# Convolution layers of a six-layer network: gates and values first, z behind them, bias masks moved into these layers

## The chip, the cores and the metric

One core of one Trainium2 chip. The metric is the device time of one launch in microseconds (us), the median of several runs. Engines: PE (TensorE), DVE (VectorE), ACT (ScalarE), POOL (GpSimd), SP (SyncE, which issues all DMAs).

## The reference, cut to what matters

Four mixer layers (convolution a0, forgetting attention b, short convolution c, convolution a1) and then two blocks of sparse and latent attention with a feed-forward part, on 256 tokens, width 1024, inner width 2048, all in float32. The change touches mostly the two convolution layers:

```
def conformer_conv_mixer(h, w_in, conv_w, conv_b, ln_g, ln_b, w_out):
    proj = h @ w_in
    val, glu_gate, z = jnp.split(proj, 3, axis=-1)
    u = val * jax.nn.sigmoid(glu_gate)
    u = causal_depthwise_conv(u, conv_w) + conv_b          # 31 taps
    u = jax.nn.silu(layer_norm(u, ln_g, ln_b))
    return (u * jax.nn.silu(z)) @ w_out
```

The later attention adds a bias looked up by the distance of two positions, `rel_bias[t5_bucket(q_pos - k_pos)]`. It depends on the positions alone, so the kernel builds it early, beside other work.

## The kernel before, in words

**Weights.** All weights stream in one fixed list of pieces of 128x1024 (512 KB) through six raw buffers. A "split" piece is cast by ACT into a high part `wh` (`feed_act`, tile wh), DVE subtracts to get the low part `wl` (`feed_dve`, tile wl), and a unit of PE work is three short-format matmuls of 256 columns for each of 8 row blocks (24 instructions, from XS and wh or wl). A "plain" piece is used by PE as it landed, in full float32: 8 matmuls that the profile shows as 16 instructions (ps<-B,raw). `LOOK = 3`: casts and subtractions run up to three pieces ahead of the unit where they are called for. SP loads piece i once piece i-6 has been used; the queue is in order.

**A convolution layer.** Channels go in eight pairs of 128-channel blocks, p = 0 to 7. For a pair there are two units each of gate (g), value (v) and z. PE makes g and v, ACT takes the sigmoid of g (`gate`), DVE multiplies (`val`, the row B<-ps,tmp), and the 31 taps follow: ACT sets up two of them, 18 are DVE multiply-adds in a PSUM bank (ps<-B,C,ps), and `POOL_TAPS = 11` go by ACT, which scales into one of three buffers (tmp<-B,C), and POOL, which adds (B<-B,tmp). Two instructions for a tap and pair, one for each block. `conv_end` (B<-ps,B) joins both sums. ACT squares the result, PE sums both over the channels (`stats`, the 128x1 matmuls). After pair 7: mean and variance on DVE (`dve_moments`) with one square root on ACT, PE spreads four columns over 128 partitions (`spread`, eight 128x128 instructions), and then DVE normalizes two blocks at a time, ACT applies silu, DVE multiplies with silu(z), ACT and DVE split the result (tile os), and PE multiplies with `w_out` (`pe_out`, 12 matmuls of 512 columns for each of 16 blocks), whose pieces are split in the same loop.

**The order**, written out by hand on each engine: PE does g0 v0, g1 v1, then g_p v_p, the sums of pair p-2 and z_(p-2) for p = 2 to 7, then z6 z7, the last sums, and the spread. g is plain, v plain for even p and split for odd p, z all split: 12 plain and 12 split pairs of units. PE's output goes round four banks, and a unit waits until the bank's last user has been read. ACT and DVE do the taps of pair p-1 in between, in a merged order of 30 items (`items(p, a, b)`; item 0 sets up). ACT loads another function table each time it goes from sigmoid to silu or back.

**The bias.** 96 masks (`masks`, DVE, 128x128), each followed by one small matmul with 32 columns (`pe_bias`, two instructions in the profile); ACT takes out a full bank of 16 (`act_bias`). Masks lie in a ring of six. 32 are made at the very start of the program, before the first layer's norm on DVE and before its transposes on PE; 64 in layer b, four for each pair of key and query units.

Lines: L103 is `matmul`, L106 `transpose`, L109 `activation`, L112 `copy` (the casts), L119 `tt`, L124 `ts`, L129 `stt`, L135 `reciprocal`.

Of the kernel before, what the change touches and what calls it, by code (L numbers as in the profile page):

```python
# [18 lines left out]
E = 2048  # L19
# [8 lines left out]
POOL_TAPS = 11  # L28
# [3 lines left out]
RING = 6  # L32
# [167 lines left out]
def plan_a(j):  # L200
    A, out = f"a{j}", []

    def two(kind, p, base, how):
        for n in range(2):
            out.append((f"{A}.{kind}{p}.{n}", tiles("a_w_in", j, base + p * 256 + 128 * n), how))

    for p in range(9):
        if p < 8:
            two("g", p, E, "plain")
            two("v", p, 0, "plain" if p % 2 == 0 else "split")  # L210
        if p == 8:
            two("z", 6, 2 * E, "split")
            two("z", 7, 2 * E, "split")
        elif p >= 2:
            two("z", p - 2, 2 * E, "split")
# [143 lines left out]
class Net:  # L359
# [85 lines left out]
    def feed_act(self, act, name):  # L445
        s = self.s
        while self.casts <= min(self.at[name] + LOOK, len(self.pieces) - 1):
# [9 lines left out]
    def feed_dve(self, dve, name):  # L457
        s = self.s
        while self.lows <= min(self.at[name] + LOOK, len(self.pieces) - 1):
# [145 lines left out]
    def pe_entry(self, pe, L, normed):  # L605

        s, idn = self.s, self.c("ident", 0, 128)
        self.warm(pe, {"a0": 0, "a1": 14, "b": 14, "c": 14, "m0": 6}.get(L, 20))
# [118 lines left out]
    def a_order(self):  # L727

        seq = []
        for p in range(9):  # L730
            if p < 8:
                seq += [("g", p), ("v", p)]
            seq += [("z", 6), ("z", 7)] if p == 8 else [("z", p - 2)] if p >= 2 else []
        bank = {x: 4 + i % 4 for i, x in enumerate(seq)}
        prior = {x: seq[i - 4] for i, x in enumerate(seq) if i >= 4}
        return bank, prior
# [6 lines left out]
    def pe_a(self, pe, j):  # L743
        s, A = self.s, f"a{j}"
        XN = self.xn()
        if j == 0:
            self.pe_bias(pe, 16, 6)
            self.pe_bias(pe, 16, 7)
# [4 lines left out]
        def pair(kind, p):  # L753
            b = self.ps[bank[kind, p]]
            if j == 0 and p == 1 and kind in "gv":
                pe.wait_ge(*s["evac"]["bias", 0 if kind == "g" else 1])
# [3 lines left out]
            for n in range(2):  # L760
                o = b[:, n * T:n * T + T]
                if kind == "g" or (kind == "v" and p % 2 == 0):
# [11 lines left out]
        for p in range(9):  # L774
            if p < 8:
                pair("g", p)
                pair("v", p)
            else:
                pair("z", 6)
                pair("z", 7)  # L780
            if p >= 2:
                stats(2 * p - 4)
                stats(2 * p - 3)
                if p < 8:
                    pair("z", p - 2)
        stats(14)
        stats(15)
        pe.wait_ge(*s["norm"][(A, "m"), "root"])
        for x in ((k, p) for k, p in bank if bank[k, p] == 7):
            pe.wait_ge(*(s["conv"] if x[0] == "v" else s["evac"])[(A,) + x])  # L790
        self.spread(pe, 7, self.m["sm"][:, 112:116], (A, "m"))
        for k in range(15):
            self.pe_out(pe, A, k, 16)
        self.pe_out_last(pe, A, [15])

    def act_a(self, act, j):
# [4 lines left out]
        if j == 0:  # L801
            self.act_rms(act, A, lambda tb, h: s[f"x{tb}"][0], "a_norm0", True)
            self.act_bias(act, 0, 6)
            self.act_bias(act, 1, 7)
# [58 lines left out]
        for p in range(9):  # L863
            at = 12 if p - 1 >= 2 else 0
            if p < 8:
                for n, (kind, m) in enumerate((("g", 0), ("g", 1), ("v", 0), ("v", 1))):
                    self.feed_act(act, f"{A}.{kind}{p}.{m}")
                    if p >= 1:
                        items(p - 1, min(30, at + 6 * n), min(30, at + 6 * n + 6))
                    if n == 1:  # L870
                        gate(p)
                if p >= 1:
                    items(p - 1, min(30, at + 24), 30)
            else:
                for n, (q, m) in enumerate(((6, 0), (6, 1), (7, 0), (7, 1))):
                    self.feed_act(act, f"{A}.z{q}.{m}")
                    items(7, min(30, at + 6 * n), min(30, at + 6 * n + 6))
                    if m:
                        silu_z(q)
                items(7, min(30, at + 24), 30)  # L880
            if p >= 2:
                stats(2 * p - 4)
                stats(2 * p - 3)
                if p < 8:
                    for m in range(2):
                        self.feed_act(act, f"{A}.z{p - 2}.{m}")
                        items(p, 6 * m, 6 * m + 6)
                    silu_z(p - 2)
# [4 lines left out]
        act.table(ACT.Silu)  # L893
        for i in range(0, 22, 2):
# [5 lines left out]
            if 2 <= i < 18:  # L900
                for k in (i - 2, i - 1):
# [3 lines left out]
                    self.act_high(act, A, k, V[:, k, :])  # L905
            for k in (i - 4, i - 3):
                if 0 <= k < 16:
                    self.feed_act(act, f"{A}.o{k}")

    def dve_a(self, dve, j):  # L910
# [4 lines left out]
        if j == 0:  # L915
            self.dve_bias_begin(dve)
            self.masks(dve, 32)
# [46 lines left out]
        for p in range(9):  # L964
            at = 12 if p - 1 >= 2 else 0
            if p < 8:
                for n, (kind, m) in enumerate((("g", 0), ("g", 1), ("v", 0), ("v", 1))):
                    self.feed_dve(dve, f"{A}.{kind}{p}.{m}")
                    if p >= 1:
                        items(p - 1, min(30, at + 6 * n), min(30, at + 6 * n + 6))  # L970
                if p >= 1:
                    items(p - 1, min(30, at + 24), 30)
                val(p)
            else:
                for n, (q, m) in enumerate(((6, 0), (6, 1), (7, 0), (7, 1))):
                    self.feed_dve(dve, f"{A}.z{q}.{m}")
                    items(7, min(30, at + 6 * n), min(30, at + 6 * n + 6))
                items(7, min(30, at + 24), 30)
            if p >= 1:
                conv_end(p - 1)  # L980
            if 2 <= p < 8:
                for m in range(2):
                    self.feed_dve(dve, f"{A}.z{p - 2}.{m}")
                    items(p, 6 * m, 6 * m + 6)
        self.dve_moments(dve, 2, E, 1e-6, s["sums"][A, 15], (A, "m"))
        dve.wait_ge(*s["spread"][A, "m"])
        mu = self.ps[7][:, 0:T].unsqueeze(1).to_broadcast([128, 2, T])
        R = self.ps[7][:, T:2 * T].unsqueeze(1).to_broadcast([128, 2, T])
        for i in range(0, 22, 2):
            if i < 16:  # L990
# [3 lines left out]
                dve.tt(a, a, R, ALU.mult).then_inc(s["norm"].up((A, "ln", i // 2)), 1)  # L994
            if 2 <= i < 18:
# [99 lines left out]
    def mask(self, n):  # L1095
        i = n % RING
        b = self.m["B"][2][:, 3392:3776] if i < 3 else self.m["sc"]
        return b[:, (i % 3) * 128:(i % 3) * 128 + 128]
# [11 lines left out]
    def masks(self, dve, n):  # L1110
# [3 lines left out]
        for _ in range(n):  # L1114
# [3 lines left out]
            if x >= RING:  # L1118
                dve.wait_ge(*s["table"][x - RING])
# [3 lines left out]
    def pe_bias(self, pe, n, bank):  # L1123
# [3 lines left out]
        for _ in range(n):  # L1127
# [3 lines left out]
            if x > 32 and x % 16 == 0:  # L1131
# [65 lines left out]
    def pe_b(self, pe):  # L1197
# [27 lines left out]
        for which in ("k", "q"):  # L1225
            for n, i in enumerate(range(0, 16, 2)):
# [11 lines left out]
                self.pe_bias(pe, 4, 3)  # L1238
# [56 lines left out]
    def act_b(self, act):  # L1295
# [23 lines left out]
        for which, dst in (("k", K), ("q", Q)):  # L1319
            for n, i in enumerate(range(0, 16, 2)):  # L1320
                if n and n % 4 == 0 or (which == "q" and n == 0):
                    self.act_bias(act, (3 if which == "q" else 2) + (1 if n and which == "q" else 0), 3)
# [12 lines left out]
        self.act_bias(act, 5, 3)  # L1335
# [32 lines left out]
    def dve_b(self, dve):  # L1368
# [72 lines left out]
        for st in range(19):  # L1441
# [1072 lines left out]
```

## Time and profile before

| | |
|---|---|
| median of 3 runs | 1984.69 us (1981.28 to 1985.75) |
| the profiled execution's own time | 1980.45 us |
| its span | 1978.7 us |
| PE busy | 1893.4 us, 96% |
| DVE busy | 1471.1 us, 74% |
| ACT busy | 1081.7 us, 55% |
| POOL busy | 308.3 us, 16% |
| mean granted clock of PE | 0.974 |

Times in rows are us from the span's start. A timeline row gives start, length, engine, line, operation, tiles out<-in, shape, count, and in brackets the idle time before it and what ended that. Matmuls overlap, so the time that one group costs PE is read from its start to the next group's start. The layers lie at: a0 from 0 to 260, b to 627, c to 862, a1 to 1108.

### The profile page before, as it was taken

How to read it: one execution, taken by the hardware profiler on the slowest of the kernel's cores; microseconds unless marked ns; L12 is line 12 of the kernel's file. 1: busy time of each engine (PE TensorE's matmuls, PEld its weight loads, DVE VectorE, ACT ScalarE, POOL GpSimd, SP SyncE). 2: the span in 40 equal slices, each digit the busy share in tenths (PEclk: the TensorE clock that was granted, in tenths of full speed). 3: DMA queues.
4: the chain of work that ended last, by engine and by line, in shares of the span. 5: the costliest groups of instructions: out<-in, count | busy, mean ns of one | idle time of the engine just before them, and what ended most of it. 6: DMA issues, size and time to landing. Idle time of an engine off the chain costs nothing.

```text
span 1978.7 us, 32775 instructions
## 1 busy us (share of the span) xinstructions
PE 1893.4 (96%) x12594; PEld 1718.5 (87%) x12594; DVE 1471.1 (74%) x2798; ACT 1081.7 (55%) x1936; POOL 308.3 (16%) x380
## 2 busy tenths in 40 slices
PE   9899899999999999998997999999999999999997
PEld 8898678887888999988996888889999898889996
DVE  7999766565676888769997677677777676677667
ACT  5788464333435444457885544546455545555554
POOL 2888000000000000008781000002000200002000
PEclk9899799998999999998997999999999999999999
DMA  5335356553444788854343454354665343445552
GB/s 210 128 139 172 115 182 224 189 166 135 148 144 165 272 300 293 302 167 153 134 171 110 162 199 147 118 186 133 220 229 176 138 144 118 137 141 175 208 190 76
DMA packets 93899, 342.23 MB, mean 173 GB/s; under 512 B 10416, under 2 KB 10672, under 8 KB 93104
## 3 DMA queue, kind: packets, MB, share of 16 engines
q1 hardware_dynamic: 93744, 340.14, 50.6%
q8 instruction: 100, 1.64, 0.3%
q14 instruction: 55, 0.45, 0.1%
HBM read 339.05 MB, written 1.05 MB: 172 GB/s over the span
## 4 chain that ended last, share of the span: by engine, by line
PE 74%; DVE 15%; ACT 9%; issue 2%; POOL 0%; DMA 0%; SPq 0%; DVEq 0%; ACTq 0%
PE ps L103 72%; DVE ps L129 5%; DVE wl L119 5%; ACT tmp L109 4%; ACT wh L112 2%; PE ps L106 1%; DVE B L119 1%; ACT B L109 1%; DVE tmp L119 1%; ACT ps L109 1%; ACT XS L112 0%; DVE X L129 0%; DVE tmp L129 0%; DVE X L119 0%; ACT os L112 0%
## 5 line engine op out<-in xcount | busy, mean ns | idle before, releaser
L103 PE MATMUL ps<-XS,wh 128*128 128x256 f32 (+1 forms) x5072 | 940.4, 287 | 4.4 <-DVE wl L119 3.2
L103 PEld LDWEIGHTS ps<-XS,wh 128*128 128x128 f32 (+1 forms) x5072 | 802.1, 193 | 12.0 <-ACT wh L112 3.5
L119 DVE TENSOR_TENSOR wl<-raw,wh 128x1024 fp32r<-128x1024 f32 (+1 forms) x493 | 601.1, 1246 | 198.6 <-ACT wh L112 198.1
L103 PE MATMUL ps<-XS,wl 128*128 128x256 f32 (+1 forms) x2536 | 722.2, 285 | 0.0
L112 ACT CAST wh<-raw 128x1024 fp32r<-128x1024 f32 (+1 forms) x493 | 494.6, 1038 | 89.1 <-PE ps L103 87.0
L103 PEld LDWEIGHTS ps<-XS,wl 128*128 128x128 f32 (+1 forms) x2536 | 490.1, 193 | 0.0
L119 POOL TENSOR_TENSOR B<-B,tmp 128x236 f32<-128x236 f32 (+10 forms) x352 | 268.3, 802 | 777.7 <-ACT tmp L109 777.7
L103 PE MATMUL ps<-wh,os 128*128 128x512 f32 x864 | 286.4, 400 | 14.3 <-DVE os L119 11.7
L129 DVE SCALAR_TENSOR_TENSOR ps<-B,C,ps 128x254 f32<-128x254 f32 (+17 forms) x576 | 224.4, 466 | 8.4 <-ACT ps L109 8.3
L103 PEld LDWEIGHTS ps<-wh,os 128*128 128x128 f32 x864 | 165.8, 192 | 50.6 <-DVE os L119 12.9
L103 PE MATMUL ps<-wl,os 128*128 128x512 f32 x432 | 171.5, 397 | 0.0
L103 PE MATMUL ps<-B,raw 128*128 128x256 f32 x768 | 168.2, 379 | 0.0
L103 PEld LDWEIGHTS ps<-B,raw 128*128 128x128 f32 x768 | 145.1, 190 | 19.2
L119 POOL TENSOR_TENSOR X<-X,B 128x512 f32<-128x512 f32 x24 | 39.8, 1675 | 706.7 <-DVE XS L119 705.8
L109 ACT ACTIVATE tmp<-B,C 128x236 f32<-128x236 f32 (+10 forms) x352 | 142.7, 477 | 8.7 <-POOL B L119 8.2
L109 ACT ACTIVATE B<-ps 128x512 f32<-128x512 f32 (+2 forms) x92 | 53.4, 586 | 164.4 <-PE ps L103 163.8
L129 DVE SCALAR_TENSOR_TENSOR tmp<-ps,C,tmp 128x254 f32<-128x254 f32 (+1 forms) x176 | 72.7, 475 | 77.4 <-ACT tmp L109 77.2
L109 ACT ACTIVATE tmp<-ps 128x384 f32<-128x384 f32 (+2 forms) x129 | 65.7, 516 | 117.1 <-PE ps L103 83.3
L129 DVE SCALAR_TENSOR_TENSOR raw<-raw,cb 128x1024 f32<-128x1024 f32 x96 | 116.3, 1216 | 0.0
L109 ACT ACTIVATE tmp<-ps,C 128x256 f32<-128x256 f32 x88 | 44.9, 561 | 120.3 <-PE ps L103 120.3
L103 PE MATMUL ps<-wh,XS 128*128 128x512 f32 x320 | 100.1, 391 | 0.0
L103 PEld LDWEIGHTS ps<-wl,os 128*128 128x128 f32 x432 | 83.2, 193 | 14.9
(157 smaller groups left out, 1855.4 us busy)
## 6 DMA issues: line engine op xcount, KB each, us to landing
raw<-in_w SPq DMA_DIRECT2D x623, 512.0 KB, 4.3
raw<-in_w SPq DMA_DIRECT2D x12, 384.0 KB, 3.7
B<-in_ln SPq DMA_DIRECT2D x4, 1024.0 KB, 6.8
C<-in_cst SPq DMA_DIRECT2D x1, 1109.5 KB, 10.3
X<-in_x SPq DMA_DIRECT2D x2, 512.0 KB, 6.1
out_x<-X SPq DMA_DIRECT2D x4, 256.0 KB, 2.5
cb<-in_cb SPq DMA_DIRECT2D x1, 512.0 KB, 12.7
raw<-in_w SPq DMA_DIRECT2D x2, 256.0 KB, 3.2
```

The costliest lines, as they stand in the source:

```text
L103: return NOTHING if self.e is None else self.e.matmul(*a, **k)
L106: return NOTHING if self.e is None else self.e.transpose(*a)
L109: return NOTHING if self.e is None else self.e.activation(*a, **k)
L112: return NOTHING if self.e is None else self.e.copy(*a)
L119: return NOTHING if self.e is None else self.e.tensor_tensor(o, a, b, op)
L129: return self.e.scalar_tensor_tensor(out=o, in0=a, scalar=s, in1=b, op0=op0, op1=op1, **k)
```

## The change

Order of the pieces and of PE in the convolution layers: g_p v_p for p = 0 to 7 and then z0 to z7. Only v0 is a plain value now, and z0 to z3 are plain. `POOL_TAPS` is 12. The sums of pair q come after v_(q+3) (one pair later than before), z6 runs between the last sums and the spread, and z7 behind the spread. The value of pair p+1 and the taps' setup no longer wait for the end of pair p's taps. 16 masks are made at the start instead of 32, 32 in a0 after the norm, 16 in layer b's attention, 32 in a1 after the norm; PE multiplies 16 of them at the start, eight after each of v1 to v4 in both convolution layers, and 16 at the start of c in place of 14 warming matmuls. Masks lie in the buffer that z will use.

```
-POOL_TAPS = 11
+POOL_TAPS = 12
+PLAIN_Z = 4
...
+    for p in range(8):
+        two("g", p, E, "plain")
+        two("v", p, 0, "split" if p else "plain")
+    for p in range(8):
+        two("z", p, 2 * E, "plain" if p < PLAIN_Z else "split")
...
+        if L == "c":
+            self.pe_bias(pe, 16, 7)
+        self.warm(pe, {"a0": 0, "a1": 14, "b": 14, "c": 0, "m0": 6}.get(L, 20))
...
         if j == 0:
             self.pe_bias(pe, 16, 6)
-            self.pe_bias(pe, 16, 7)
...
+        for p in range(8):
+            pair("g", p)
+            pair("v", p)
+            if 1 <= p < 5:
+                self.pe_bias(pe, 8, 3)
+            if p >= 3:
+                stats(2 * p - 6)
+                stats(2 * p - 5)
+        for p in range(6):
+            pair("z", p)
+            if p in (1, 4, 5):
+                q = {1: 5, 4: 6, 5: 7}[p]
+                stats(2 * q)
+                stats(2 * q + 1)
+        pair("z", 6)
         pe.wait_ge(*s["norm"][(A, "m"), "root"])
...
+        pe.wait_ge(*s["evac"][A, "z", 3])
         self.spread(pe, 7, self.m["sm"][:, 112:116], (A, "m"))
+        pair("z", 7)
```

On ACT (DVE has the same pattern, with `val(p + 1)` after item 20, `conv_end(p - 1)` after item 8, and `masks(32)` ahead of the first value):

```
+        gate(0)
+        self.feed_act(act, f"{A}.v1.0", 1)
+        for p in range(8):
+            items(p, 0, 4)
+            if p < 6:
+                self.feed_act(act, f"{A}.v{p + 2}.0", 0)
+            if p in (2, 4):
+                self.act_bias(act, (4 if j else 1) + (p == 4), 3)
+            if p == 7:
+                silu_z(2)
+                self.feed_act(act, f"{A}.z4.0", 1)
+            items(p, 4, 10)
+            if p < 7:
+                gate(p + 1)
+            else:
+                silu_z(3)
+                self.feed_act(act, f"{A}.z5.0", 1)
+            items(p, 10, 14)
...
+            if p == 6:
+                silu_z(0)
+            items(p, 14, 18)
+            if p:
+                stats(2 * p - 2)
+                stats(2 * p - 1)
+            items(p, 18, 22)
+            if p == 6:
+                silu_z(1)
...
+        silu_z(4)
+        self.feed_act(act, f"{A}.z7.0", 0)
         stats(14)
         stats(15)
...
+        self.feed_act(act, f"{A}.z7.1", 0)
+        silu_z(5)
+        self.feed_act(act, f"{A}.o0", 1)
+        silu_z(6)
...
+            if i == 4:
+                silu_z(7)
```

In the output loop of DVE `feed_dve(o0, i // 2)` is added for i = 0 and 2: the first pieces of `w_out` used to be split before the loop. Layer b loses `pe_bias(4, 3)`, `masks(4)` and four `act_bias`, and gets `masks(4)` for the heads 9 to 12 between `maxima` and `dve_quotients`.

## Rows read from the trace of the kernel before

**Rows 1.** The page, part 4: the chain that ended last, by engine.

```profile
PE 74%; DVE 15%; ACT 9%; issue 2%; POOL 0%; DMA 0%; SPq 0%; DVEq 0%; ACTq 0%
```

**Rows 2.** Windows: stretch, busy PE, PEld, DVE, ACT, POOL, granted clock, DMA share, GB/s.

```profile
882.30:1048.10 165.80, 154.40 (x1008) 145.88 (x1006) 154.49 (x330) 135.30 (x289) 134.12 (x176) 0.96 0.43 150
66.10:76.30 10.20, 8.19 (x38) 8.19 (x39) 8.62 (x22) 6.69 (x18) 6.79 (x12) 0.50 0.13 50
376.70:383.50 6.80, 6.80 (x33) 6.80 (x33) 5.99 (x12) 0.89 (x1) 0.00 (x0) 0.50 0.91 317
```

**Rows 3.** Timeline of PE in a0: sums, a split pair, two plain pairs.

```profile
91.67 0.50 PE L103 MATMUL ps<-C,B 128*128 128x1 f32 x4
...
93.37 0.48 PE L103 MATMUL ps<-XS,wh 128*128 128x256 f32 x2
...
99.21 13.98 PE L103 MATMUL ps<-B,raw 128*128 128x256 f32 x64
```

**Rows 4.** Timeline of PE in a1: first units; spread; output.

```profile
868.25 20.88 PE L103 MATMUL ps<-B,raw 128*128 128x256 f32 x96
...
1053.45 2.07 PE L103 MATMUL ps<-C,sm 128*128 128x128 f32 x8 [1.73 <-DVE sm L129]
1060.22 0.80 PE L103 MATMUL ps<-wh,os 128*128 128x512 f32 x1 [4.70 <-DVE os L119]
```

**Rows 5.** Timeline of the program's start on PE, DVE and ACT.

```profile
4.12 1.46 PE L103 MATMUL ps<-C,B 128*128 128x32 f32 x6 [4.12 <-DVE B L124]
...
17.98 3.65 PE L106 MATMUL ps<-C,tmp 128*128 128x128 f32 x16
...
3.63 0.85 DVE L124 TENSOR_SCALAR B<-B,C 128x128 f32<-128x128 f32 x3
...
15.70 0.16 DVE L124 TENSOR_SCALAR sm<-sm 128x2 f32<-128x2 f32 x1
...
29.36 0.34 DVE L124 TENSOR_SCALAR rope<-rope,C 32x256 f32<-32x256 f32 x1
...
9.75 0.19 ACT L109 ACTIVATION_READ_ACCUMULATOR tmp<-X 128x1 f32 x1
```

**Rows 6.** Timeline of DVE in a1: first pair's taps, then a low part.

```profile
884.35 13.80 DVE L129 SCALAR_TENSOR_TENSOR ps<-B,C,ps 128x254 f32<-128x254 f32 x36 [0.26 <-ACT ps L109]
...
903.34 1.67 DVE L119 TENSOR_TENSOR wl<-raw,wh 128x1024 fp32r<-128x1024 f32 x1 [0.45 <-ACT wh L112]
```

**Rows 7.** Timeline of POOL in a1: the adds of pairs 0 and 1.

```profile
885.52 14.07 POOL L119 TENSOR_TENSOR B<-B,tmp 128x236 f32<-128x236 f32 x22 [685.72 <-ACT tmp L109]
901.30 15.97 POOL L119 TENSOR_TENSOR B<-B,tmp 128x236 f32<-128x236 f32 x22 [1.71 <-ACT tmp L109]
```

**Rows 8.** Timeline of ACT in a1: table for silu, (silu left out), cast, scaled taps.

```profile
1008.27 1.28 ACT L109 ACT_TABLE_LOAD   x1
...
1010.06 1.04 ACT L112 CAST wh<-raw 128x1024 fp32r<-128x1024 f32 x1
1010.99 1.62 ACT L109 ACTIVATE tmp<-B,C 128x232 f32<-128x232 f32 x4
```

**Rows 9.** Timeline of DVE in the output loop of a0.

```profile
208.99 2.73 DVE L119 TENSOR_TENSOR B<-B,ps 128x512 f32<-128x512 f32 x4 [2.17 <-PE ps L103]
...
223.09 0.76 DVE L119 TENSOR_TENSOR os<-B,os 128x256 fp32r<-128x256 f32 x2 [0.86 <-ACT os L112]
...
253.38 0.76 DVE L119 TENSOR_TENSOR os<-B,os 128x256 fp32r<-128x256 f32 x2 [0.47 <-ACT os L112]
```

**Rows 10.** Timeline of PE in layer b: sums, next sums; then the mask wait.

```profile
342.22 1.04 PE L103 MATMUL ps<-tmp,C 128*16 128x256 f32 x4
...
350.03 1.04 PE L103 MATMUL ps<-tmp,C 128*16 128x256 f32 x4
...
376.38 0.86 PE L103 MATMUL ps<-C,sc 128*128 128x32 f32 x4 [1.80 <-DVE sc L124]
```

**Rows 11.** Timeline of DVE in layer b's attention: the wait where masks go.

```profile
547.96 0.17 DVE L135 RECIPROCAL sm<-sm 128x2 f32<-128x2 f32 x1 [0.98 <-ACT tmp L109]
```

More of the change, by code:

```diff
@@ L443, in sp_program, with feed_act @@
         sp.wait_ge(s["out"].sem, 64)
-    def feed_act(self, act, name):
+    def feed_act(self, act, name, look=LOOK):
         s = self.s
-        while self.casts <= min(self.at[name] + LOOK, len(self.pieces) - 1):
+        while self.casts <= min(self.at[name] + look, len(self.pieces) - 1):
             i = self.casts
@@ L727, in a_order @@
     def a_order(self):
[L729 to L733, printed above, removed]
+        seq = [(kind, p) for p in range(8) for kind in "gv"] + [("z", p) for p in range(8)]
         bank = {x: 4 + i % 4 for i, x in enumerate(seq)}
         prior = {x: seq[i - 4] for i, x in enumerate(seq) if i >= 4}
+        bank["z", 7], prior["z", 7] = 4, ("z", 4)
         return bank, prior
@@ L754, in pair @@
             b = self.ps[bank[kind, p]]
-            if j == 0 and p == 1 and kind in "gv":
-                pe.wait_ge(*s["evac"]["bias", 0 if kind == "g" else 1])
+            if j == 0 and p == 1 and kind == "g":
+                pe.wait_ge(*s["evac"]["bias", 0])
             if (kind, p) in prior:
@@ L761, in pair @@
                 o = b[:, n * T:n * T + T]
-                if kind == "g" or (kind == "v" and p % 2 == 0):
+                if kind == "g" or (kind, p) == ("v", 0) or (kind == "z" and p < PLAIN_Z):
                     self.plain_unit(pe, o, f"{A}.{kind}{p}.{n}", XN, A)
@@ L861, in stats @@
                 s["square"].up((A, i)), 1)
[L863 to L873, printed above, removed]
-            else:
[L875 to L888, printed above, removed]
+        gate(0)
[12 more added lines that the diff above has]
+                gate(p + 1)
+            else:
+                silu_z(3)
+                self.feed_act(act, f"{A}.z5.0", 1)
+            items(p, 10, 14)
+            if p < 6:
+                self.feed_act(act, f"{A}.v{p + 2}.1", 0)
+            if p == 6:
[7 more added lines that the diff above has]
+                silu_z(1)
+            if p == 7:
+                self.feed_act(act, f"{A}.z6.0", 0)
+            items(p, 22, 30)
+        silu_z(4)
+        self.feed_act(act, f"{A}.z7.0", 0)
         stats(14)
@@ L962, in val @@
                    ALU.mult).then_inc(s["conv"].up((A, "v", p)), 1)
[L964 to L979, printed above, removed]
-                conv_end(p - 1)
[L981 to L984, printed above, removed]
+        self.masks(dve, 32)
+        self.feed_dve(dve, f"{A}.v1.0", 1)
+        val(0)
+        for p in range(8):
+            items(p, 0, 8)
+            if p:
+                conv_end(p - 1)
+            if p < 6:
+                self.feed_dve(dve, f"{A}.v{p + 2}.0", 0)
+            if p == 7:
+                self.feed_dve(dve, f"{A}.z4.0", 1)
+            items(p, 8, 14)
+            if p == 7:
+                self.feed_dve(dve, f"{A}.z5.0", 1)
+            items(p, 14, 20)
+            if p < 7:
+                val(p + 1)
+            if p < 6:
+                self.feed_dve(dve, f"{A}.v{p + 2}.1", 0)
+            items(p, 20, 28)
+            if p == 7:
+                self.feed_dve(dve, f"{A}.z6.0", 0)
+            items(p, 28, 30)
+        conv_end(7)
+        self.feed_dve(dve, f"{A}.z7.0", 0)
         self.dve_moments(dve, 2, E, 1e-6, s["sums"][A, 15], (A, "m"))
+        self.feed_dve(dve, f"{A}.z7.1", 0)
         dve.wait_ge(*s["spread"][A, "m"])
```

59 lines of the change are left out of this document (17 added, 42 removed).

## The prediction

> **What bounds the kernel now.** I read the chain of waits by engine first: PE holds three quarters of the chain, DVE a seventh [rows 1]. The windows by stage then show where PE isn't the bound: in the taps' stretch of a convolution layer PE and DVE are both busy 154 of 165.8 us and POOL 134 [rows 2]. The timeline of PE shows what DVE and ACT cost it at the end of the layer, 1.73 us before the spread and 4.70 before the output [rows 4]; a window of a0 with 2.0 of 10.2 us idle is wholly at half clock [rows 2], as are others behind pauses. So a gain comes from filling these pauses with z, as long as the taps on DVE, ACT and POOL end in time, and from work that PE no longer does. I work with the profiled execution, 1980.45 us; it lies 4.2 under the median of the runs, so gains are taken off the median at the end.
>
> **Prices on PE.** A split pair of units costs 5.84 us, start to start, after a plain one about 5.9; a plain pair 6.90 (two take 13.98, overlap of 0.17 left out); the sums of a pair 1.70 [rows 3]. In layer b the period is 7.81 [rows 10], of which 5.9 are units and 1.0 are the norm's sums; the four masks' matmuls have the rest, 0.9.
>
> **Layer b.** 16 groups of four masks' matmuls go. 15 of them give 0.9 each, 13.5. The sixteenth stands behind the 1.80 us wait for a mask, and after it PE runs at half clock for 6.8 us [rows 2, 10], which costs 3.4: with the matmuls themselves (about 1.0 at that clock) 6.2, less 0.3 that PE will then wait for the low part of the next units. Sum 19.4. ACT loses four evacuations and DVE 64 masks there; both have slack. The 16 masks that come back in the attention stand where DVE now waits 0.98 us for ACT [rows 11]; four masks take 4 x 0.26 = 1.04 (0.85 for three that overlap [rows 5]). Hidden but for 0.1 a head if DVE has no other slack; all of it, 4.2, if it has none; I take 0.4. Layer b: 19.0 less time; bounds 14 and 20. In c, 16 masks' matmuls (3.6 us at 0.9 for four) replace 14 warming ones of about the same length: 0, between -1 and +1; ACT's one more evacuation hides behind PE's split units.
>
> **The start of a0.** 32 masks' matmuls hold PE from 4.12 to 17.98, 0.43 each [rows 5]. 16 end at 11.1. The norm could start when ACT has its squares, 9.75 + 0.19, but DVE makes masks until 15.70 [rows 5]; with 16 masks it is ready at 3.6 + 16 x 0.26 = 7.8. The norm comes 5.8 us earlier, and so PE's first unit, now at the end of the transposes, 21.4: 15.6. If the full clock comes no earlier than now, PE runs its first units at half speed until about 21.7 and loses 3.0; if it comes as long after the transposes as now, nothing. I take 1.5. But DVE now makes 32 masks (8.2) and two low parts (2.4) before it multiplies the first value: norm and rope are done at 29.7 - 5.8 = 23.9 [rows 5], so the first value is ready at 35.2, against 36.3 now. Of the 5.8 us PE keeps all, the taps 1.1. In a1 the masks fit where DVE idles while PE makes g0 and v0, but for about 0.5.
>
> **PE's ledger of a convolution layer.** Now 12 plain and 12 split pairs, then 13 and 11: +1.0. The masks' matmuls add eight groups of four at 0.85: +6.8. From the first unit to the end of z3: 13 plain pairs 89.7, seven split 41.3, six sums 10.2, masks 6.8: 148.0. From there z4 5.9, sums 1.7, z5 5.9, sums 1.7, z6 5.9, spread 1.0.
>
> **The taps.** DVE: 36 multiply-adds take 13.80 [rows 6], 34 take 13.0; value and join 1.2; two low parts of 1.2 to 1.67 [rows 6]: about 17 a pair against 20.7 now (165.8 / 8 [rows 2]). POOL: 22 adds take 14.07 with no low part in between, 0.64 each, and 15.97 with two, so a low part on DVE costs POOL 0.95 [rows 7]. 24 adds and two low parts: 15.4 + 1.9 = 17.3. The Trainium skill, SBUF — State Buffer, section "SBUF: two separate sides", says that DVE operations with two SBUF inputs and POOL operations shut each other out for a whole instruction. By that rule a low part would cost POOL all its 1.22 or so, and a layer's 17 low parts 4.6 us more than by the rows; I keep the rows.
> ACT: 24 scaled taps at 0.39 [rows 8], 9.3, setup 2.1, gate 0.6, two casts 1.9, squares 0.7: 14.6. It loses about 11 table loads of 1.28 [rows 8] a layer, since the gates are together. So POOL and DVE set 17.3 a pair, and POOL is ready for pair 7 at: a1, first add 0.5 later than 885.52 [rows 7], + 6 x 17.3 + 15.4 (pair 6 has no low part) = 1005.
>
> **What is late next.** In pair 7 ACT waits for silu of z2 after item 4 and of z3 after item 10, in order, ahead of the taps that POOL needs. In a1 PE starts at 868.3 [rows 4], so z3 ends at 868.3 + 148.0 = 1016.3, 11 us after POOL could start pair 7. Then ACT: silu 0.5, two casts 1.9, the next scaled taps 0.8 [rows 8]: 1019.5. POOL has 16 adds and three low parts left: 10.2 + 2.9 = 13.1, so 1032.6. Join 0.7, the rest of the squares and PE's sums 2.0: 1035.3; z6 5.9, spread 1.0: the layer norm starts at 1042.2. Now it starts at 1053.45 + 2.07 = 1055.5 [rows 4]. Gain 13.3. In a0 the same chain from 15.6 + 1.5 + 148.0 = 165.1 gives 191.0 against 208.99 [rows 9]: 18.0.
>
> **The output loop.** PE has z7 for the 4.70 us pause, and the half clock behind it goes. But the first splits of w_out moved into DVE's loop: one at i = 0, one at i = 2, three instead of two at i = 4, 1.2 each, and ACT has silu of z7 and one more cast at i = 4. Followed through, the third pair of os comes 4.1 later than 223.09 - 208.99 = 14.1 behind the norm's start, and the period after it stays 6.4, as now. The last pair starts 44.4 + 4.1 = 48.5 behind it [rows 9]; with its first half's 0.4 and two blocks on PE (2 x 2.72 at full clock) the output ends at 54.3. Now it ends at 51.4 (PE's 16 blocks from 4.7 on, 3.2 of it lost to half clock). Cost 2.9 a layer; between 0, if PE sets the end, and 4.4.
>
> **Sum.** Layer b 19.0, a0 18.0 - 2.9, a1 13.3 - 2.9: 44.5. 1980.45 - 44.5 = 1936.0, and 1984.69 - 44.5 = 1940.2 for the median. Its own range, from the bounds above: 1930 to 1951.
>
> **Rivals.** (A) PE alone sets the pace: ACT's stall in pair 7 is covered by what POOL still has buffered. Then the norm starts at PE's ledger, 148.0 + 22.1 after the first unit: 1038.4 and 187.2, 3.8 less each: 1932.6. For it: three buffers between ACT and POOL. Against: they hold 3 x 1.3 us of adds, the stall is 11.
> (B) Half clock at the tail. PE pauses about 4 us before the last sums of a1 (ready at 1031, taps done at 1033.5) and 1 to 3 in the output loop. The pause of 1.80 was followed by 6.8 us at half clock, and 10.2 is the longer kind [rows 2, 10]. Two such stretches a layer, 4 us each at the end: +8 to +16, 1952. The Trainium skill, TensorE: Matmul & The Clock Gate, section "What's actually happening", has it that the engine is throttled by default and activity releases it; by this rule the pauses count, the trace agrees.
> (C) Slower than before: the half clock comes with every pair. PE's 14.6 to 15.5 us of work a pair lie inside a tap period of 17.3, and if the slack is taken as one pause of 2 us before each pair's sums, and each brings 10.2 us at half clock (5.1 lost), 12 of them cost 61: 2002. It decides from nine such pauses on (44.5 / 5.1). Against: in a1 PE starts behind the taps and reaches each sum later than they do.
> (D) Layer b gives less: with the masks gone PE waits at the same place for low parts or weights (three pieces of 512 KB in 7 us are 225 GB/s, under the 317 of a busy stretch [rows 2]). Then only 8 of its 19 us come: 1951.
> (E) The start gives nothing, since PE waits for the taps anyway: +4; within the range.
>
> **How the numbers follow.** The forecast 0.5, A 0.2, B 0.18, C 0.03, D 0.07, others above 1960 0.02. The range takes in A with the lower bounds of the output loop and of layer b (1932.6 - 2 x 2.9 - 1 = 1926, and 2 for the start's clock: 1924) and B with its 16 us and the upper bound of the attention's masks (1956 + 4): 1924 to 1960. About 0.2% (4 us) is what a measurement of this kernel can tell from no change. Faster 0.95, same 0.02, slower 0.03.
>
> **What would show it.** Right: layer b's key and query period on PE 6.9 instead of 7.81 and no 1.80 wait; first unit on PE near 15.6; the start of the layer norm near 191 in a0 and near 1042.2 - 34 = 1008 in a1 (a0 and b come first); on ACT an idle stretch before the silu of z2 and z3 in pair 7, and on POOL idle time there in place of the idle time at each pair's start; the output loop's end 54 behind the norm's start. Wrong: half clock inside the taps' stretch (C), POOL's adds above 0.75 each throughout, or PE waits on low parts in layer b (D).

## The result and the profile after the change

| | before | after |
|---|---|---|
| median | 1984.39 us (4 runs, 1981.28 to 1985.75) | 1957.32 us (4 runs, 1951.40 to 1963.19) |
| the profiled execution | 1980.45 us | 1957.44 us |

The ratio is 0.9866, 95% interval 0.9834 to 0.9898: 27 us faster by the medians, 23 by the two profiled executions. The forecast was 44.5, to 1940.2. By stages of the two profiled executions, each from the last stage's end to its own:

| stage | forecast | measured | short of the forecast |
|---|---|---|---|
| a0, to the end of its output (260.34, now 254.33) | -15.1 | -6.0 | 9.1 |
| b (to 627.16, now 602.75) | -19.0 | -18.4 | 0.6 |
| c | 0 | 0.0 | 0 |
| a1 (862.14 to 1106.94, now 837.73 to 1081.09) | -10.4 | -1.4 | 9.0 |
| the two blocks behind | 0 | +2.7 | 2.7 |

So both convolution layers lack 9 us. The windows of the kernel after show where: first the two stretches from the first unit to the end of z3 (where z4 starts), then those at half clock inside them and the one before a0's spread. Columns as in [rows 2].

```profile
15.30:172.98 157.68, 155.85 (x914) 143.33 (x913) 144.38 (x340) 119.70 (x275) 124.23 (x175) 0.96 0.43 139
843.84:999.72 155.88, 154.62 (x915) 142.37 (x913) 140.07 (x328) 116.24 (x272) 123.77 (x175) 0.96 0.41 132
...
75.80:82.60 6.80, 6.80 (x26) 6.08 (x26) 6.80 (x17) 6.37 (x15) 6.80 (x11) 0.50 0.00 0
96.30:103.10 6.80, 6.80 (x21) 5.72 (x21) 6.80 (x16) 4.69 (x12) 6.80 (x11) 0.50 0.00 0
901.90:912.10 10.20, 10.20 (x36) 9.03 (x36) 10.20 (x23) 8.06 (x20) 10.20 (x14) 0.50 0.01 2
925.80:929.20 3.40, 3.40 (x10) 2.65 (x9) 3.40 (x7) 2.46 (x8) 3.40 (x5) 0.51 0.00 0
191.90:195.30 3.40, 3.40 (x18) 3.40 (x18) 1.42 (x6) 3.26 (x5) 0.00 (x0) 0.50 0.77 245
```

From first unit to z4 PE takes 157.7 and 155.9 where the prediction had 149.5 and 148.0. 13.6 us at half clock in each cost half of that, 6.8. The timeline of PE in the kernel after shows the rest: the start; the masks' matmuls behind v3, where the bank of 16 is full until ACT takes it out; those behind v4; the last sums; and the spread and the output.

```profile
3.90 7.01 PE L103 MATMUL ps<-C,B 128*128 128x32 f32 x32 [3.90 <-DVE B L124]
...
15.30 7.02 PE L103 MATMUL ps<-B,raw 128*128 128x256 f32 x26
...
73.89 2.63 PE L103 MATMUL ps<-C,B 128*128 128x32 f32 x20 [1.83 <-ACT B L109]
...
93.51 2.29 PE L103 MATMUL ps<-C,B 128*128 128x32 f32 x20
95.66 0.58 PE L103 MATMUL ps<-C,tmp 128*128 128x1 f32 x4
96.11 0.81 PE L103 MATMUL ps<-C,B 128*128 128x1 f32 x4
...
189.24 0.61 PE L103 MATMUL ps<-C,B 128*128 128x1 f32 x4 [2.63 <-DVE B L119]
...
198.37 1.05 PE L103 MATMUL ps<-C,sm 128*128 128x128 f32 x8
206.01 0.50 PE L103 MATMUL ps<-wh,os 128*128 128x512 f32 x1 [0.84 <-DVE os L119]
```

To be seen: the first unit stands at 15.30 against 21.4 [rows 5]. The half clock from 75.8 on stands just behind the pause that ends at 73.89; the stretch from 96.3 on has no pause ahead of it, only eight masks' matmuls and the sums (93.51 to 97.6). a1 has the same pair: 1.25 us of waiting for ACT at 900.62, half clock from 901.9 and again from 925.8. The 1.73 and 4.70 of [rows 4] are gone; in their place PE waits 2.63 for the last join of the taps, at 189.24 and at 1015.98, and 0.84 before the output.

POOL in pairs 6 and 7 of a0, kernel after:

```profile
151.91 5.10 POOL L119 TENSOR_TENSOR B<-B,tmp 128x232 f32<-128x232 f32 x8 [2.53 <-ACT tmp L109]
158.81 3.79 POOL L119 TENSOR_TENSOR B<-B,tmp 128x228 f32<-128x228 f32 x6 [1.81 <-ACT tmp L109]
...
169.40 4.73 POOL L119 TENSOR_TENSOR B<-B,tmp 128x236 f32<-128x236 f32 x6 [5.05 <-ACT tmp L109]
176.31 12.05 POOL L119 TENSOR_TENSOR B<-B,tmp 128x233 f32<-128x233 f32 x16 [2.18 <-ACT tmp L109]
```

and ACT, the silu of z2 and of z3, which stand ahead of the scaled taps that POOL lacks:

```profile
166.46 0.60 ACT L109 ACTIVATE B<-ps 128x512 f32<-128x512 f32 x1 [3.13 <-PE ps L103]
...
173.36 0.60 ACT L109 ACTIVATE B<-ps 128x512 f32<-128x512 f32 x1 [2.13 <-PE ps L103]
```

In layer b the 1.80 us wait of [rows 10] is gone; one of 0.50 for a low part is left. The sums of two key and query units stand at 346.42 and 353.33, 6.9 apart against 7.81:

```profile
346.42 1.04 PE L103 MATMUL ps<-tmp,C 128*16 128x256 f32 x4
353.33 1.04 PE L103 MATMUL ps<-tmp,C 128*16 128x256 f32 x4
...
362.06 0.47 PE L103 MATMUL ps<-XS,wh 128*128 128x256 f32 x2 [0.50 <-DVE wl L119]
```

### The profile page after: what moved, and what is told of

The parts are those of the page before. It is cut to its first block, busy times and chain, and to the rows that moved or that the text cites. A ratio compares the mean times of both kernels' runs of the same rounds, so it can differ in the third digit from the quotient of the medians.

```text
span 1955.6 us, 32679 instructions
## 1 busy us (share of the span) xinstructions
PE 1889.9 (97%) x12534; PEld 1707.9 (87%) x12534; DVE 1451.4 (74%) x2762; ACT 1067.0 (55%) x1944; POOL 314.4 (16%) x412
## 4 chain that ended last, share of the span: by engine, by line
PE 74%; DVE 11%; ACT 8%; issue 5%; POOL 1%; DMA 0%; SPq 0%; DVEq 0%; ACTq 0%; POOLq 0%
PE ps L103 73%; DVE wl L119 4%; ACT tmp L109 3%; ACT wh L112 2%; POOL B L119 1%; DVE B L119 1%; PE ps L106 1%; ACT B L109 1%; DVE tmp L119 1%; DVE B L124 1%; ACT os L112 1%; DVE tmp L129 0%; DVE X L129 0%; ACT XS L112 0%; ACT ps L109 0%
## 5 line engine op out<-in xcount | busy, mean ns | idle before, releaser
L103 PE MATMUL ps<-XS,wh 128*128 128x256 f32 (+1 forms) x5008 | 927.1, 287 | 4.9 <-DVE wl L119 3.7
L103 PEld LDWEIGHTS ps<-XS,wh 128*128 128x128 f32 (+1 forms) x5008 | 790.4, 193 | 18.2 <-issue 7.5
L103 PE MATMUL ps<-XS,wl 128*128 128x256 f32 (+1 forms) x2504 | 711.9, 284 | 0.0
L103 PEld LDWEIGHTS ps<-XS,wl 128*128 128x128 f32 (+1 forms) x2504 | 482.8, 193 | 0.0
L119 POOL TENSOR_TENSOR B<-B,tmp 128x237 f32<-128x237 f32 (+11 forms) x384 | 274.4, 755 | 740.2 <-ACT tmp L109 740.2
L129 DVE SCALAR_TENSOR_TENSOR ps<-B,C,ps 128x254 f32<-128x254 f32 (+16 forms) x544 | 211.9, 471 | 21.6 <-ACT ps L109 21.2
L103 PE MATMUL ps<-B,raw 128*128 128x256 f32 x832 | 194.2, 395 | 0.0
L103 PEld LDWEIGHTS ps<-B,raw 128*128 128x128 f32 x832 | 164.2, 199 | 23.6
L109 ACT ACTIVATE tmp<-B,C 128x237 f32<-128x237 f32 (+11 forms) x384 | 160.6, 478 | 32.6 <-POOL B L119 32.2
```

Of the source, the lines that this page charges most:

```text
L103: return NOTHING if self.e is None else self.e.matmul(*a, **k)
L109: return NOTHING if self.e is None else self.e.activation(*a, **k)
L119: return NOTHING if self.e is None else self.e.tensor_tensor(o, a, b, op)
L129: return self.e.scalar_tensor_tensor(out=o, in0=a, scalar=s, in1=b, op0=op0, op1=op1, **k)
```

## The experiments

The medians below were taken in groups, each beside the kernel before on the same chip (medians 1982.5, 1984.7 and 1983.5; the last repeat with 11 taps stands alone, one execution beside one of 1984.3); ratios are to that. Each trace is of one execution.

**The base.** No edit.

> The changed kernel once more, unchanged, as the base for the runs beside it. Expected 1957 (1951 to 1963), by every theory. In the profile: two stretches at half clock between the first value and the end of z3 in each convolution layer, and one pause of 1 to 2 us of PE for ACT before the third group of masks' matmuls.

Median 1956.2 (1953.7 to 1964.9), ratio 0.9856 (0.9836 to 0.9876). Pauses for ACT of 2.54 and 1.37, half clock at 74.5 and 98.4, 910.8 and 931.2: the pattern repeats, but not the lengths. Half clock takes 10.2 and 6.8 us in a0 here and 6.8 and 6.8 in a1, where the first trace had 6.8 and 6.8, and 10.2 and 3.4.

**The masks' matmuls elsewhere.** On PE they move from behind v_p to between g_p and v_p, one pair later. Theories 1 to 3 are told in the expectation.

```
+            if 2 <= p < 6:
+                self.pe_bias(pe, 8, 3)
             pair("v", p)
-            if 1 <= p < 5:
-                self.pe_bias(pe, 8, 3)
```

> The masks' matmuls of the convolution layers move from behind v1 to v4 to between g and v of the pairs 2 to 5. ACT has then taken out the first bank long before PE wants it, and the masks' matmuls no longer stand directly ahead of the channel sums. Theory 1 (the missing time is what the masks' matmuls bring with them: a pause for ACT of 1.83 and 1.25 us and stretches at half clock, 13.6 us of them in each layer, behind the pause and behind masks and sums in one run): the stretches between first value and z3 go, z3 ends at 164.3 in a0 instead of 172.98, and the kernel gains 1.83 + 6.8 + 1.25 + 6.8 = 16.7, less 0 to 4 if the taps then set the end: 1941 to 1945. Theory 2 (only the pause brings half clock, and the second stretch comes from the taps' work or the time since the start): the second stretch stays, 3.4 and 1.7 us, gain about 11: 1946. Theory 3 (the placing of the masks' matmuls does nothing; PE is slower there for the weights' stream or the taps): the stretches stay, gain 0 to 3: 1954 to 1957.

Median 1963.2 (1956.0 to 1976.7), ratio 0.9899 (0.9871 to 0.9928): no gain, rather a loss, which none of the three theories had. The pauses for ACT went, but PE now waits for low parts: 5.67 at 74.05, 2.19 at 124.87, 0.51 at 141.55, and 2.18 and 3.28 in a1. The wait of 5.67 stands behind one low part that took 9.08 us on DVE (last section), so a0 of this execution says little; a1 has none such. From the first unit to z4 a0 took 160.1 and a1 156.0, where the kernel after had 157.7 and 155.9. So in a1 something else than the pause holds PE in this stretch.

**The bank taken out sooner.**

```
+            if p in (2, 4):
+                self.act_bias(act, (4 if j else 1) + (p == 4), 3)
             items(p, 0, 4)
             if p < 6:
                 self.feed_act(act, f"{A}.v{p + 2}.0", 0)
-            if p in (2, 4):
-                self.act_bias(act, (4 if j else 1) + (p == 4), 3)
```

> Only ACT's taking out of the bias bank moves: at the start of pairs 2 and 4 ahead of the first four tap items and the casts instead of behind them. The pause of PE before the third group of masks' matmuls (1.83 in a0, 1.25 in a1) goes or is halved; the run of thin matmuls (eight masks, then the sums of a pair) stays. Theory 1 (such a run alone is followed by half clock): the stretches stay, perhaps shorter by 3.4 us each, gain 2 to 6: 1951 to 1955. Theory 2 (the pause brings the half clock): the stretch behind the pause goes in both layers, gain 1.8 + 1.3 + 3.4 + 5.1 = 11.6: 1946.

Median 1956.1 (1953.8 to 1958.9), ratio 0.9859 (0.9838 to 0.9880): nothing gained, which neither theory had. Both pauses for ACT are gone, and at their places half clock still comes, 3.4 us in a0 and 6.8 in a1. The kernel after had 6.8 and 10.2 there, its repeat 10.2 and 6.8; so half clock comes without the pause, and what the pause adds is not shown by one trace each. The second stretch of a0 now begins at 136.0, inside a wait of PE. In v6 and v7 of a0 new waits stand, PE's timeline:

```profile
119.12 0.47 PE L103 MATMUL ps<-XS,wh 128*128 128x256 f32 x2 [2.02 <-DVE wl L119]
136.44 0.76 PE L103 MATMUL ps<-XS,wh 128*128 128x256 f32 x2 [2.65 <-DVE wl L119]
```

This gave **theory L**: up to v7 PE is tied to DVE. The second low part of v(p+2) is made behind the value of pair p+1, at item 20 of pair p, so it keeps the taps' pace. What PE saves is spent waiting there, as soon as PE is ahead of it.

**The order alone, masks as before.** Ring of six, 32 at the start, `pe_bias(4, 3)` back in layer b, none in a0's and a1's loops. This undoes one half of the change.

> Only the new order of the convolution layers and the 12 taps; bias masks, their matmuls and their evacuations where they were before (32 at the start, 64 in layer b, ring of six). Layer b is as before (+18.4), PE's first unit at 21.4 instead of 15.3 and the first value near 36.3 instead of 34.1. Theory L (until z3 PE is held by the second low parts of v6 and v7, which stand in DVE's queue behind the value of the next pair; the masks' matmuls, their pause and their half clock only fill time in which PE would have waited): the convolution layers hardly gain from losing the masks, z3 ends at 173 to 175 in a0 and 155 after the first unit in a1, PE waits 2 to 8 us for low parts in v5 to v7; 1957 + 18.4 + 2 - 3 = 1974 (1970 to 1978). The prediction's ledger (PE's own work alone): masks' matmuls 6.8, pause and half clock about 8 less in each layer, 14 to 15 gained in a1 and 9 in a0: 1957 + 18.4 - 24 = 1951.

Median 1975.2 (1972.1 to 1977.0), ratio 0.9948 (0.9928 to 0.9968): theory L had 1974, the ledger alone 1951. So the new order and the twelfth tap alone gain 9.5 beside their own kernel before, and some 17 to 18 of the 27 come from the moved masks. PE's timeline in a0, every row with a wait between 86 and 142 us:

```profile
88.69 0.47 PE L104 MATMUL ps<-XS,wh 128*128 128x256 f32 x2 [2.65 <-DVE wl L120]
106.00 0.47 PE L104 MATMUL ps<-XS,wh 128*128 128x256 f32 x2 [2.65 <-DVE wl L120]
123.31 0.47 PE L104 MATMUL ps<-XS,wh 128*128 128x256 f32 x2 [2.64 <-DVE wl L120]
140.62 0.47 PE L104 MATMUL ps<-XS,wh 128*128 128x256 f32 x2 [2.64 <-DVE wl L120]
```

and DVE beside it, without an idle row:

```profile
103.72 0.68 DVE L120 TENSOR_TENSOR B<-ps,tmp 128x512 f32<-128x512 f32 x1
104.32 1.54 DVE L120 TENSOR_TENSOR wl<-raw,wh 128x1024 fp32r<-128x1024 f32 x1
105.78 7.86 DVE L130 SCALAR_TENSOR_TENSOR ps<-B,C,ps 128x243 f32<-128x243 f32 x20
113.55 0.68 DVE L120 TENSOR_TENSOR B<-ps,B 128x512 f32<-128x512 f32 x1
114.15 1.60 DVE L120 TENSOR_TENSOR wl<-raw,wh 128x1024 fp32r<-128x1024 f32 x1
115.67 5.43 DVE L130 SCALAR_TENSOR_TENSOR ps<-B,C,ps 128x250 f32<-128x250 f32 x14
121.03 0.67 DVE L120 TENSOR_TENSOR B<-ps,tmp 128x512 f32<-128x512 f32 x1
```

The waits are 17.31 apart, as the values on DVE are: PE's slack is taken once in each pair, in front of one low part. The masks' matmuls in the changed kernel mostly fill this time.

**The second low part sooner**, on top of the early evacuation; on DVE:

```
             if p == 7:
                 self.feed_dve(dve, f"{A}.z5.0", 1)
+            if p < 6:
+                self.feed_dve(dve, f"{A}.v{p + 2}.1", 0)
             items(p, 14, 20)
             if p < 7:
                 val(p + 1)
-            if p < 6:
-                self.feed_dve(dve, f"{A}.v{p + 2}.1", 0)
```

> The kernel with ACT's early evacuation of the bias bank (the pause of PE for ACT is gone in it, and PE waits 2.0 and 2.65 us for low parts in v6 and v7 of a0 instead), and on DVE the second low part of v(p+2) at item 14 of pair p instead of behind the value at item 20, about 3 us sooner. Theory L (low parts hold PE until z3): these waits go, z3 ends 2.5 to 3 us sooner in a0 and 0.4 to 1.5 in a1, and with it silu of z3, the taps' end and the norm: 1956 - 3 to 5 = 1951 to 1953. If the clock or the taps' own pace held PE there: the waits turn into others, 1955 to 1957.

Median 1948.7 (1946.4 to 1955.7), ratio 0.9824 (0.9802 to 0.9846): 7 us less than without the moved low part, more than the 3 to 5 expected. By the traces the stretch to z4 is 3.7 shorter in a0 (156.5 to 152.8) and 2.9 in a1 (153.4 to 150.45). a0 has no wait for a low part any more, a1 two of 1.13. In a1 the last unit of v7 follows its low part at once in both kernels, at 962.01 and now at 959.08 with the same first unit, so the half clock of 10.2 that a1 had without the moved low part had only filled time of waiting. Its windows from first unit to z4, and the two stretches at half clock in a0:

```profile
15.33:168.17 152.84, 152.84 (x913) 140.81 (x913) 143.07 (x340) 119.69 (x275) 124.27 (x175) 0.97 0.44 144
842.59:993.04 150.45, 148.19 (x915) 136.98 (x913) 139.18 (x328) 116.50 (x272) 123.85 (x175) 1.00 0.43 137
...
73.50:80.30 6.80, 6.80 (x22) 5.72 (x22) 6.80 (x14) 6.67 (x17) 6.43 (x9) 0.50 0.00 0
94.00:97.40 3.40, 3.40 (x9) 2.65 (x10) 3.40 (x9) 3.24 (x8) 3.40 (x6) 0.50 0.00 0
```

**Silu later on ACT.** z0 moves to item 22 of pair 6, z1 to item 10 of pair 7, z2 behind the taps, z3 and z4 behind the root:

```
-                silu_z(2)
                 self.feed_act(act, f"{A}.z4.0", 1)
...
-                silu_z(3)
+                silu_z(1)
                 self.feed_act(act, f"{A}.z5.0", 1)
...
             if p == 6:
-                silu_z(1)
+                silu_z(0)
...
-        silu_z(4)
+        silu_z(2)
         self.feed_act(act, f"{A}.z7.0", 0)
...
+        silu_z(3)
         self.feed_act(act, f"{A}.z7.1", 0)
+        silu_z(4)
```

> ACT takes silu of z0 to z4 later (z0 at item 22 of pair 6, z1 at item 10 of pair 7, z2 behind pair 7's taps, z3 and z4 behind the norm's root), so that no scaled tap is queued behind a z unit of PE. By the prediction's step (ACT's stall in pair 7 sets the end of the taps): the waits of ACT of 2 to 3 us go, POOL's idle time of 11.6 us in pairs 6 and 7 of a0 goes, the last sums no longer wait for DVE (2.63 in each layer) and the half clock behind that pause (3.4 us, 1.7 lost) goes too: 4.3 a layer, 1957 - 8.6 = 1948 to 1949. By the rival (the taps themselves are too slow, POOL's and DVE's own 17.3 us a pair): the join of pair 7 stays where it is, the pause of 2.6 us too, gain 0 to 2: 1955 to 1957.

Median 1948.9 (1946.0 to 1949.8), ratio 0.9820 (0.9799 to 0.9840): 7.3 less than the base, as the prediction's step had it. The last sums start without a wait in both layers, and the half clock before the spread is gone. POOL's idle time in pairs 6 and 7 of a0, which was to go, only fell from 12.0 to 7.4. But this execution has one low part of 9.10 us on DVE (last section), behind which PE waited 4.66 at 73.63; z3 ended late because of it and the norm still began 1 us sooner than in the kernel after.

**All of it**, and the two first low parts of `w_out` ahead of the norm's loop:

```
+        self.feed_dve(dve, f"{A}.o0", 1)
         dve.wait_ge(*s["spread"][A, "m"])
...
-            if i < 4:
-                self.feed_dve(dve, f"{A}.o0", i // 2)
```

> All of it: silu of z later (alone 1949), early evacuation of the bias bank, second low parts at item 14, and the two first low parts of w_out ahead of the layer norm's loop instead of inside it. Theory L: z3 3 us sooner in a0 and 1 in a1, but the taps' own pace then sets the end (17.3 a pair, seven pairs and 13 us from the first add), so 0 to 3 a layer of it show; the output loop 2.4 to 3.5 shorter in each layer, 54.9 to 52. Sum 1949 - 6 - 2 = 1941 (1937 to 1945). If a low part on DVE is again held up for 5 to 9 us by POOL's adds: up to 5 more, 1946.

Median 1937.5 (1936.6 to 1942.4), ratio 0.9767 (0.9745 to 0.9790): 18 us under the changed kernel by the two ratios, 47 under the one before. The moved low parts of `w_out` had little part in it, 0.7 a layer where 2.4 to 3.5 was expected. From the spread to the output's end it is, in a0, 189.94 to 245.22, 55.3, against 56.0. DVE's timeline in a0 says why:

```profile
188.02 1.23 DVE L119 TENSOR_TENSOR wl<-raw,wh 128x1024 fp32r<-128x1024 f32 x1 [2.09 <-ACT wh L112]
189.94 2.36 DVE L119 TENSOR_TENSOR wl<-raw,wh 128x1024 fp32r<-128x1024 f32 x2 [0.70 <-ACT wh L112]
192.22 2.72 DVE L119 TENSOR_TENSOR B<-B,ps 128x512 f32<-128x512 f32 x4
```

ACT's first cast for them is done only at 189.9, when PE's spread is already starting; the two low parts no longer stand inside the loop but directly ahead of it.

**A gap for DVE on POOL**, on top of all of it:

```
+                if p < 6 and k in (8, 5):
+                    pool.wait_ge(*s["low"][self.at[f"{A}.v{p + 2}.{int(k == 5)}"]])
```

> As the one with all of it, and POOL waits before its fourth and seventh tap of the pairs 0 to 5 until DVE has made the low part that stands there. Theory S (a low part on DVE gets no turn while POOL's adds follow each other without a gap: one took 9.10 us in one run, in which POOL did 12 adds on end): with the wait every low part of these pairs takes 1.2 to 1.7 us, none over 2. POOL idles about 1.2 for each, little more than the 0.95 it loses now: 0 to 4 us slower or faster than without, 1938 to 1945. Rival (the long low part came from the weights' stream or a late cast): long ones can appear here too.

Median 1937.5 (1936.4 to 1941.9), ratio 0.9767 (0.9745 to 0.9788). The same time, and no long low part in the convolution layers, but the kernel without the wait had none either: it costs nothing and shows nothing.

**11 taps.** `POOL_TAPS = 11` in the changed kernel.

> The changed kernel with 11 taps on ACT and POOL, as before the change, so that DVE makes 18 multiply-adds for each block instead of 17. Theory L (DVE's time for a pair is the pace, 17.3, and PE follows it through the low parts): a pair takes 2 x 0.38 more, 18.1; PE gets waits for low parts and the norm starts 5 to 6 later in each layer: 1957 + 10 to 12 = 1967 to 1969. If POOL set the pace, a pair gets shorter (two adds of 0.64 less) and the kernel 0 to 8 faster: 1950 to 1957. If PE's own work set it: 1957, no change.

Median 1961.6 (1952.2 to 1967.2), ratio 0.9899 (0.9878 to 0.9919); the profiled execution is the one of 1952.2. In it a pair of taps takes 17.3 from value to value, as with 12. My 18.1 was wrong: with 11 taps POOL has some slack (it waits 1.21 for ACT at 104.94), and DVE's low parts mostly take 1.2 to 1.35 instead of 1.45 to 1.65:

```profile
99.44 1.21 DVE L119 TENSOR_TENSOR wl<-raw,wh 128x1024 fp32r<-128x1024 f32 x1
...
108.78 1.20 DVE L119 TENSOR_TENSOR wl<-raw,wh 128x1024 fp32r<-128x1024 f32 x1
```

Of what the two added multiply-adds cost, 0.8, the shorter low parts give back 0.4 to 0.6; DVE's idle time for ACT in three of the pairs of the kernel after (0.67 to 1.30) is gone too. So the twelfth tap did not change the pace in this execution. The median is another matter: it lies between what the three theories had, 5 us over the base's 1956.2 and 8.5 by the ratios, and the pace doesn't explain that.

**Repeats for the long low part.** The kernel with silu later unchanged, the same with POOL waiting (as above, before taps 8 and 3), and the one with 11 taps again.

> The kernel with silu of z later, once more, unchanged, to see whether its one low part of 9.10 us on DVE (pair 1 of a0, DVE in line behind 12 of POOL's adds) comes again. Time as before, 1949 (1946 to 1952). If the place decides, a low part of over 5 us stands at the same place in this profile; if it hangs on the moment in which DVE and POOL meet, it may be gone or elsewhere.

> The same, and POOL waits for the low part in the pairs 0 to 5 before the tap that stands beside it, which gives DVE a gap between two adds. If POOL's row of adds is what holds the low part up: none of over 2 us in the pairs 0 to 5, 1945 to 1950. If something else holds it up (a late piece of weights, a late cast), a long one can appear all the same.

> The kernel with 11 taps once more. Its profiled execution took 1952.2, the four others 1961 to 1967. If the difference comes from low parts on DVE that get no turn beside POOL's adds, an execution near 1961 shows one or more of over 5 us in the convolution layers, which the one at 1952 did not (longest 1.7); if it comes from half clock or from the weights' stream, the low parts are all short and the clock's list or the stretches of other layers are longer.

Silu later again: 1946.0 (2 runs), no low part over 1.8 in the convolution layers: the place alone does not decide. With the gap: 1945.1 (2 runs), none either, which shows nothing of the gap. 11 taps again: 1954.75, longest 3.10 at 91.59. None caught an execution near 1961, so the 9 to 15 us by which four of the executions with 11 taps were longer stay unexplained.

## Why the prediction was right in direction and too large

The measured 1957.3 lies in the range, 1924 to 1960, at its upper end, 17 over the forecast of 1940.2. That it lies inside is in part luck: the width on that side was kept for half clock at the tail, and two other things used it.

**The sum of PE's work was right; what held PE was not only its work.** The ledger had 148.0 from first unit to z4. Time less waits and less half of what ran at half clock (with the low part sooner the full clock came at 15.5, so a0's start lost nothing):

| kernel, layer | taken | waits | clock | left |
|---|---|---|---|---|
| after, a0 | 157.7 | 1.8 | 6.8 + 1.2 at the start | 147.9 |
| after, a1 | 155.9 | 1.25 | 6.8 | 147.8 |
| low part sooner, a0 | 152.8 | 0 | 5.1 | 147.7 |
| low part sooner, a1 | 150.45 | 2.3 | 0 | 148.2 |
| order only, a1 (no masks: 148.0 - 6.8 = 141.2) | 152.6 | 10.9 | 0 | 141.7 |

The step that failed is "From the first unit to the end of z3 ... 148.0" as the time at which z3 ends; it took 157.7 and 155.9. It left out two things. First, v6's and v7's low parts, which stand in DVE's queue behind five pairs of taps at 17.3: with the bank taken out sooner PE waited for them in a0 (2.65 at 136.44), and z4 could not come before about 136.4 + 2.9 + 1.7 + 14.0 + 1.7 + 14.0 = 170.7, where I had 165.1. Of a0's 7.9 us at z4, 5.6 would thus have been lost without any pause or half clock. In a1 the same sum from 962.01 gives 996.3, 5.7 later than 148.0 behind the first unit at 842.6. The text named low parts as a risk for layer b only, in (D). Second, the masks' matmuls at 0.85 for four, with nothing around them: they brought pauses of 1.83 and 1.25 for ACT, and behind them 6.8 us were lost at half clock in each layer. Without these matmuls (order only) a1 had no half clock in this stretch and a0 3.4 us. These two aren't added: each fills time that the other would take, which is why removing the pauses alone gave nothing (1956.1), and only together with the low part 7 us. Why the clock falls at the masks' matmuls stays open.

**Layer b, right.** 18.4 for 19.0; period 6.9, no 1.80, and one wait of 0.50 for a low part where I had 0.3. **c, right**, 0.0. **The start of a0, right**: first unit 15.30 for 15.6, first value 34.09 for 35.2, clock lost 1.2 for 1.5.

**The taps' pace, right in size, wrong in its reason.** 17.3 on POOL and DVE alike; with 11 taps it is 17.3 too. The rows of DVE in the order-only kernel show it without an idle row at 12 taps, so a low part's extra 0.3 to 0.4 beside POOL counts on DVE, where I had it on POOL only.

**ACT's stall in pair 7, right.** From z4 to the norm's start a1 took 26.4 for the predicted 25.9. With silu later it took 22.1 in both layers (a0: 176.4 to 198.47), exactly rival A's chain behind the ledger. So A was wrong for this kernel, and its 3.8 a layer were there to be had: 7.3 were measured for both. **The output loop, right**: 54.9 for 54.3 in both layers. **Rival B** held in part: the pause before the last sums (2.63; I had written about 4, though my own dates, 1031 and 1033.5, give 2.5) was followed by 3.4 us at half clock, 1.7 lost and not 4. **Rival C** had half clock inside the taps, which the prediction named as a sign of being wrong, and it came, at two places a layer; it cost 13.6 in both layers together. Its mechanism, a pause before each pair's sums, did not come: PE never waited for sums in this stretch. Where its slack was taken as a pause of 2.65 in each pair (order only), it stood before a low part, and one of eight such waits had half clock behind it. **Rival D** and (E) did not come.

**The blocks behind**, +2.7: 13.6 us at half clock there against 10.2, at other places. That is 1.7 of it; the remaining 1.0 is open.

## What to carry to other kernels

When a ledger of one engine is to give a date, check for each operand that another engine makes in order (here a low part queued behind a value) when that engine gets to it, and take the later of both. Moving work into an engine's slack is worth it where the slack is, and the order-only run shows that it was here: from a layer's first unit to its output's end the masks add 1.2 in a0 (239.0 against 237.8) and 3.3 in a1 (237.3 against 234.0), where layer b is 18.4 shorter than before. And a result that is taken early (silu of z) in an in-order queue holds up all that stands behind it: put it just ahead of the unit that needs its bank.

## What the runs showed of the hardware that was not expected

**A low part on DVE can be held for many of POOL's adds.** In the kernel after, a low part on DVE and an add on POOL that meet both take longer. DVE:

```profile
64.71 1.50 DVE L119 TENSOR_TENSOR wl<-raw,wh 128x1024 fp32r<-128x1024 f32 x1
```

and the add that POOL had in the queue meanwhile, 1.66 instead of 0.67:

```profile
65.09 1.66 POOL L119 TENSOR_TENSOR B<-B,tmp 128x230 f32<-128x230 f32 x1
```

In the kernel with silu later, at the same place, DVE and then POOL:

```profile
64.38 9.10 DVE L119 TENSOR_TENSOR wl<-raw,wh 128x1024 fp32r<-128x1024 f32 x1
```

```profile
65.40 6.99 POOL L119 TENSOR_TENSOR B<-B,tmp 128x230 f32<-128x230 f32 x11
...
72.85 1.17 POOL L119 TENSOR_TENSOR B<-B,tmp 128x236 f32<-128x236 f32 x1 [0.46 <-ACT tmp L109]
```

POOL's adds follow each other at 0.64 as if DVE were not there, and the low part ends 1.09 after POOL's first idle time, which began at 72.39. The cast that this low part needs had ended on ACT at 60.06, so neither it nor the piece of weights was late. It happened so in two of the thirteen traces since the change (9.10 here and 9.08 with the masks' matmuls elsewhere, both in pair 1 of a0), with shorter ones of 5.24 and 3.10 besides in convolution layers; what decides it is open. The Trainium skill, SBUF — State Buffer, section "SBUF: two separate sides", calls this port pair an exclusive lock that whichever starts first has for the whole instruction. The rows agree with that for one instruction. That the waiting one may lose its turn twelve times running, the page doesn't say, and the rows show it. The prediction kept 0.95 for each low part and held the rule against it; 1.66 - 0.67 = 0.99 is what one add lost here.

**Half clock without a pause.** In the kernel with the low part sooner PE has no wait over 0.3 us in a0 from its first unit to z4, and the granted clock still falls to 0.50 (1.2 GHz) from 73.5 and from 94.0. The timeline of PE ahead of it:

```profile
70.78 2.29 PE L103 MATMUL ps<-C,B 128*128 128x32 f32 x20
72.94 0.58 PE L103 MATMUL ps<-C,tmp 128*128 128x1 f32 x4
73.38 0.87 PE L103 MATMUL ps<-C,B 128*128 128x1 f32 x4
74.11 0.99 PE L103 MATMUL ps<-C,tmp 128*128 128x1 f32 x4
74.97 7.22 PE L103 MATMUL ps<-B,raw 128*128 128x256 f32 x20
```

The fall at 73.5 lies inside this stretch of matmuls with 32 and 1 columns (70.78 to 74.97), the one at 94.0 just behind the next such stretch (90.36 to 93.85); PE counts as busy throughout. In a1 the same sequence had no fall in that run. So these matmuls and the falls go together in a0, and no run shows that they are the cause. Five waits of up to 2.66 us in a1 of the order-only kernel, each before a unit of 256 columns, had none behind them: its window from 868.33 on has a granted clock of 1.00. In a0 of that kernel one of the four such waits had, 3.4 us from 142.1.

```profile
868.33:1020.94 152.61, 141.68 (x850) 130.08 (x849) 132.71 (x296) 114.94 (x270) 123.86 (x175) 1.00 0.43 135
```
